# The transposed x operands at another place within 256 bytes, and the weight slots that meet them

## The reference

```
z = x @ w_in + b_in                                   # 1024 -> 8192 columns
z_pool, z_lru, z_b, z_c, z_h, z_gate = split(z)
y_pool = multiscale_pool(z_pool, pool_w, pool_scale)
y_lru  = rg_lru(z_lru, ...) @ lru_w_out
y_conv = gated_short_conv(z_b, z_c, z_h, sconv_w, sconv_w_out)
gates  = sigmoid(z_gate)                              # three of 1024 columns
x = LN(ALPHA * x + (g0*y_pool + g1*y_lru + g2*y_conv) @ w_mix_out)
x = LN(ALPHA * x + cross_attention(x, mem, 256 memory tokens, 4 heads))
x = LN(ALPHA * x + (silu(x @ w_gate) * (x @ w_up)) @ w_down)   # 2816 wide
```

## Time and profile before

| | us |
|---|---|
| median of 3 runs | 1020.75 |
| lowest and highest | 1012.27 and 1020.95 |
| the profiled execution | 1019.84 |
| its span | 1017.9 |
| mean granted clock, share of full speed | 0.996 |

### The profile page before, as it was taken

One profiled execution on the slowest core, in us unless ns is written; L12 is line 12 of the kernel. 1 busy time (PEld: TensorE's weight loads), 2 busy tenths in 40 slices (PEclk: granted clock), 3 DMA queues, 4 the chain that ended last, 5 costly groups with the idle time before them and its releaser, 6 DMA issues.

```text
span 1017.9 us, 15708 instructions
## 1 busy us (share of the span) xinstructions
PE 998.7 (98%) x6460; PEld 910.0 (89%) x6460; DVE 715.7 (70%) x893; ACT 501.7 (49%) x710; POOL 49.6 (5%) x47
## 2 busy tenths in 40 slices
PE   8999999999899999999999999999999999999997
PEld 8888889898899998888889998889999999988885
DVE  5979797896898876455765554679878878742336
ACT  6573737556575663223544442457454554532232
POOL 1010000101000000000310000040000000000000
PEclk9999999999999999999999999999999999999999
DMA  8043433316233353225163331233424332333212
GB/s 311 28 157 107 145 109 124 120 62 199 91 106 105 104 178 114 102 82 207 49 201 124 124 125 42 83 104 105 125 84 125 107 101 83 128 122 117 89 42 83
DMA packets 91397, 117.46 MB, mean 115 GB/s; under 512 B 3244, under 2 KB 82240, under 8 KB 91328
## 3 DMA queue, kind: packets, MB, share of 16 engines
q1 hardware_dynamic: 87648, 103.82, 31.6%
q0 software_dynamic: 3536, 12.61, 3.5%
q10 hardware_dynamic: 144, 0.05, 0.0%
HBM read 111.23 MB, written 5.24 MB: 114 GB/s over the span
## 4 chain that ended last, share of the span: by engine, by line
PE 82%; DVE 9%; ACT 6%; issue 3%; POOL 0%; DVEq 0%; ACTq 0%; POOLq 0%
PE ps L867 27%; PE ps L869 27%; PE ps L868 27%; DVE wl L1989 1%; DVE v L2039 1%; PE ps L896 1%; ACT wh L1487 1%; ACT wh L1431 1%; DVE xnat L1971 1%; DVE o L2170 1%; DVE wl L2183 0%; DVE xT_l L1921 0%; ACT ps L1417 0%; PE ps L1184 0%; POOL wl L818 0%
## 5 line engine op out<-in xcount | busy, mean ns | idle before, releaser
L867 PE MATMUL ps<-xT_h,wh 128*128 128x256 f32 (+1 forms) x512 | 170.6, 333 | 3.1 <-DVE wl L1989 1.5
L868 PE MATMUL ps<-xT_l,wh 128*128 128x256 f32 (+1 forms) x512 | 169.8, 332 | 0.0
L869 PE MATMUL ps<-xT_h,wl 128*128 128x256 f32 (+1 forms) x512 | 169.7, 332 | 0.0
L1913 DVE TENSOR_TENSOR wl<-raw,wh 128x1024 fp32r<-128x1024 f32 x58 | 70.5, 1223 | 112.9 <-ACT wh L1375 112.9
L1375 ACT ACTIVATE wh<-raw 128x1024 fp32r<-128x1024 f32 x66 | 69.2, 1060 | 151.6 <-PE ps L869 143.5
L2183 DVE TENSOR_TENSOR wl<-raw,wh 128x1024 fp32r<-128x1024 f32 x72 | 87.5, 1223 | 56.8 <-ACT wh L1487 56.5
L1487 ACT ACTIVATE wh<-raw 128x1024 fp32r<-128x1024 f32 x72 | 75.4, 1057 | 101.6 <-PE ps L869 65.1
L867 PE MATMUL ps<-wh,st_h 128*128 128x512 f32 x304 | 118.8, 391 | 0.0
L869 PE MATMUL ps<-wh,st_l 128*128 128x512 f32 x304 | 118.3, 389 | 0.0
L868 PE MATMUL ps<-wl,st_h 128*128 128x512 f32 x304 | 118.3, 389 | 0.0
L867 PEld LDWEIGHTS ps<-xT_h,wh 128*128 128x128 f32 x512 | 96.3, 188 | 13.0 <-issue 1.7
(11 more groups left out here) (302 smaller groups left out, 2420.8 us busy)
## 6 DMA issues: line engine op xcount, KB each, us to landing
raw<-in_w_in SPq DMA_DIRECT2D x42, 512.0 KB, 3.9
raw<-in_ffn_w_down SPq DMA_DIRECT2D x11, 1024.0 KB, 4.9
raw<-in_ffn_w_gate SPq DMA_DIRECT2D x20, 512.0 KB, 4.0
wx<-in_w_in SPq DMA_DIRECT2D x16, 512.0 KB, 4.6
gb<-in_ffn_w_up SPq DMA_DIRECT2D x10, 512.0 KB, 4.1
raw<-in_ffn_w_up SPq DMA_DIRECT2D x10, 512.0 KB, 4.5
raw<-in_lru_w_out SPq DMA_DIRECT2D x8, 512.0 KB, 3.5
raw<-in_sconv_w_out SPq DMA_DIRECT2D x8, 512.0 KB, 3.4
```

The source lines that it names most:

```text
L867: nc.tensor.matmul(dst, st, mv_, start=start, stop=False, skip_group_check=shared)
L868: nc.tensor.matmul(dst, st, mv_lo_part, start=False, stop=False, skip_group_check=shared)
L869: return nc.tensor.matmul(dst, st_lo_part, mv_, start=False, stop=stop, skip_group_check=shared)
L1913: nc.vector.tensor_tensor(w_slot(wl, phase, s, size), src, w_slot(wh, phase, s, size).bitcast(F32), ALU.subtract).then_inc(w_lo.sem, 1)
```

## The change

A tile of 192 bytes, `to_xT`, is placed ahead of `xq` and `xT_h` and takes the place of `to_xa`, which was in the scope of `xa` alone. So `xq`, `xT_h` and `xT_l` begin 192 bytes past a multiple of 256, and `xa` stays where it was. The tile behind `xT_l` shrinks from 256 to 64 bytes, so that `raw` and all tiles behind it keep their addresses. `w_at` is changed with it: the lru, pool and b units from step 2 on (not `pool_w` and `ri`) have their weights at 48 elements, the products on `xT` have theirs at 0, and in the attention q goes from 0 to 48. The pairs afterwards are: 256-column products on `xT` (192, 0), the 512-column units on `xT` (192, 192); the others are as before.

```
@@ -118,14 +118,14 @@
         row_sum = sb("row_sum", [P, TT])
         inv_sum = sb("inv_sum", [P, TT])
         sb("to_1k", [P, SMALL_PAD])
+        sb("to_xT", [P, 48])
         with ExitStack() as scope:
-            sb("to_xa", [P, 48], F32, scope)
             xa = sb("xa", [P, 8, 4, 256], F32R, scope)
         with ExitStack() as scope:
             xq = sb("xq", [P, KT, SEQ], F32, scope)
         xT_h = sb("xT_h", [P, KT, SEQ], F32R)
         xT_l = sb("xT_l", [P, KT, SEQ], F32R)
-        sb("past_xa", [P, 64])
+        sb("past_xT", [P, 16])
         raw = sb("raw", [P, RAW_SLOTS, 2048])
@@ -374,12 +374,10 @@
         def w_at(phase, s):
 
             n = FIRST[phase] + s
-            if n < B0:
-                return 16 if n < 2 or A_ORDER[n % A_BODY] in ("P1", "P2", "P3") else 0
-            if n < C0:
-                return 16 if n - B0 in [b_step(m, name) for m in range(B_SETS) for name in ("P1", "P2", "P3")] else 0
+            if 2 <= n < B0:
+                return 48 if A_ORDER[n % A_BODY][:-1] in ("lru", "pool", "b") else 0
             if D0 <= n < E0:
-                return (16, 48, 0)[(n - D0) // 2 % 3]
+                return (16, 48, 48)[(n - D0) // 2 % 3]
             return 0
```

## The result

| | before | after |
|---|---|---|
| median of 15 runs each, us | 1020.62 | 1011.52 |
| lowest and highest, us | 1010.80 and 1020.96 | 1010.31 and 1020.18 |
| the profiled execution, us | 1019.84 | 1010.91 |
| its span, us | 1017.9 | 1009.1 |

The ratio is 0.9941, with a 95% interval of 0.992 to 0.9963. The median is 9.5 us under the forecast of 1021 and 0.5 us under the lower end of the range.

What follows compares the result with a forecast made beforehand. TensorE bounds the kernel (busy 998.7 of 1017.9 us), by number of matmuls times pace. Terms sum to +0.6 on the profiled 1019.84, 1020.4; plus 0.9 to the median, 1021.3, said as 1021; range 1012 to 1025.

Steps and rivals of the forecast that it cites:

- Step (1): 256-column `xT` products lose their seams: passes three and four +0.6 us, one and two 0, gates 0 (-1.6 to +1.6).
- Step (2): 720 matmuls of 512 columns on `xT`, from (0, 0) to (192, 192): 0, bounds -9.6 and +6.6 us.
- Rival C: 512-column matmuls at 192 pay for straddling 256-byte blocks in passes and attention q: +3.0 to +6.6 us; chance 0.10.
- Step (3): Everything else, such as writes into `xT` and weight slots and loads into `xq`, costs nothing.
- Step (4): FFN stage's pace level, no address changed: taken as profiled, 0; -7.0 us if it stayed short.
- rival B: FFN stage keeps its short level in the median run: -7.0 us, giving 1014; chance 0.17.
- Rival A: Uniform 256-column stream is short, also behind 512-column units: -4.5 us, giving 1016; chance 0.15.
- Rival D: Matmul time beyond the column count, on `xT`, comes from placement and vanishes: -18.7 us, giving 1002; chance 0.03.
- Rival E: The change alters nothing in the kernel: 1020.75 us; chance 0.03.

## Why the prediction was wrong, and where it was right

**Step (1), the seams: right.** The `xT`, `ta` and `tb` matmuls of the gate stage have one mean. It is 276, the short end, and that end was priced at -1.6: 126.24 to 124.58 is -1.66. P5 to P7 of passes three and four became long: 13.85 to 14.14 us for five products, twice 0.29 is +0.6, as said. Passes one and two, put at 0 and bounded at 0.4 each way, came out 0.7 shorter, outside the bound. This was no change of pace between 113 and 117.8 ns but the clock in the first pass, which the prediction, going by the page's slices, had at its upper level throughout. It was luck: in the second profiled execution of the same kernel the clock fell as before. That the tile has no part was shown with everything at (0, 64), and that a seam alone makes it was shown with `xc`. The long end appears as well: 1012.4 (the lower group of before) plus 1.6 plus 0.6 is 1014.6, and the three middle executions are at 1014.07 to 1015.01; 1012.4 less 1.66 plus 0.6 is 1011.3, and the ten lowest are at 1010.31 to 1011.61. That these groups are the gates' two levels is worked out from sizes; no execution of the middle group was profiled on the kernel after itself; the two profiles with the gates long and the FFN short are of variants with a cost of their own, at 1015.73 (`xc` at 0) and 1015.23 (the wide units at 192 and 0), and those with both short, this kernel twice and two variants, are at 1010.91 to 1011.95.

**Step (2), 512 columns at (192, 192): right**, 0, with 226.7 ns a matmul on both sides. Rival C (the straddling) is dead by this, for this pair. The 6.6 us of its upper end is not far from the 4.8 that a difference of 192 costs, but the change keeps the difference at 0.

**Step (3): right.** Outside passes, gates and FFN no stage differs by more than 0.17 us.

**Step (4), the FFN's level: the step that failed.** I took it as in the profile, long, at 0, and gave the short level (rival B) 0.17, because "that is a minority" of three or four runs. It is a draw of each execution, and a median says only which side has more than half. Of before, 4 in 15, 22 in 35, 24 in 35, 12 in 29 and 16 in 23 executions were short; the median of before itself moved between 1012.44 and 1020.62 from one comparison to the next. The -7.0 of that step was well sized: 186.60 to 179.52 is -7.08. Rival B named mechanism and place; with its 1014.3 (1021.3 less 7.0), less 1.66 for the gates, it gives 1012.6, against 1011.52. Most of the rest is the 0.9 that was added to reach the median of before: that median stood in the upper group, so its offset does not go with a short FFN. From the profiled 1019.84 the same terms give 1019.84 + 0.6 - 7.1 - 1.7 = 1011.6. The short execution that was shown, 1012.27, said the same: with +0.6 and -1.6 it gives 1011.3. The forecast should have stood on both levels with near even chances, and its lower end on the short executions; the 1012 at which the range ended left the case of gates and FFN both short just outside.

**Rival A** (the uniform stream short behind 512 columns) did not happen: P1 is long at 155.35. **Rival D** (the excess is the placement's) is dead: no difference gave less than 113.3 ns. (Its two terms, 9.65 and 9.14, add up to 18.8, not 18.7.) **Rival E** is refuted by the gate stage.

**Does the change shift the FFN's draw?** After had 2 of 15 and 2 of 12 in the upper group, before 11 of 15 and 11 of 35 beside them. The first pair points to yes, the second is no clear difference. With the two variants on that chip which leave the FFN's addresses alone and add nothing (`q_sum` first, the wide units at 192 and 0) it is 6 of 36 against 24 of 70: the same direction, not clear of chance either. And the same stage gave 11 of 12 with everything at (0, 64), so the program around it does shift the draw. What does it was not shown, and so it stays open how much of the 9.1 us belongs to the change and would come again. What does belong to it by the traces is the gates' and the passes' part, some -1 us with the gates short and +2 with them long.

**A version to keep:** the kernel after with the two extra matmuls, 1012.21, ratio 0.9962 (0.9937 to 0.9987). Its median is no better than the 1011.52 and 1011.77 of the kernel after, but none of its twelve executions is in the upper group: its highest is 1013.48, and the mean of its twelve executions 1012.2, where those of the kernel after have 1012.9 and 1013.0 (in other comparisons). In the four variants with the FFN's extra matmul, none of 48 executions is above 1017.

## What to carry to other kernels

When the few times shown of a kernel stand in two groups, find the stretch in which their distance fits (here 66 units by 24 by 4.4 ns), and treat its state as a draw with its own chance, not as a property of the median. A float32r stream of 256-column matmuls at one pair of remainders keeps the level that it met, short or long: made uniform, the gates were worth -1.7 us in one profile and would be worth +1.6 at the long level, so uniformity alone is no gain. A stream that a wait can throw long can be set short again by one matmul at another pair, of 0.12 us here, placed behind the waits; it turned the FFN in two profiles and the gates in one. Of the two differences tried with 512 columns, equal remainders are the faster.

## What the runs showed of the hardware that I had not expected

- At a granted clock of 1.00, a 256-column float32r matmul takes, by moving less weight address mod 256: 0, 120.0 ns; 64, 113.3 or 117.6; 128, 118.6; 192, 113.3 or 117.6. With 512 columns: 0, 226.7; 192, 233.3. At 256 columns the values for 0 and 128 are from one pair each, (192, 192) and (192, 64), in one execution.
- At difference 192 the level lasts: once long behind the late start of the earlier trace rows, it was kept for 184 us and 1,564 matmuls; at 64 it was kept as long in the runs at (192, 128).
- A late start need not change it: one of 0.16 us from start to start left the FFN long, one of 0.22 left it short.
- The same wait of some 2.3 us was followed by the lower level of the clock in two of the three traces shown and not in the third. Over the sixteen traces of all runs, the first pass took 59.7 to 60.0 us in the eleven that have it, and 59.1 to 59.2 in the five that do not.
- A single 256-column matmul at (0, 64) between matmuls at (192, 0), though it has the same difference of 192, ends a long level, as the step from (0, 64) to (192, 0) does in the earlier trace rows; there the step back makes the unit long.
- Wide units at (192, 0) are slower by 6.6 ns and leave a short level behind them; at (192, 192) or (0, 0) they are at their best and leave a long one. The last unit alone does not decide it.
